# Side-by-side heads in the second block's attention, and buffers rounded up to 128 bytes, in a kernel of two transformer blocks

## What is computed

```python
for qb in range(s_len // Q_BLOCK):                  # Q_BLOCK = 128, two blocks
    start = qb * Q_BLOCK; end = start + Q_BLOCK
    z = jnp.einsum('bqhd,bkhd->bhqk', qi, kj) * scale   # keys 0 to end
    causal = s_pos < t_pos
    log_beta = jax.nn.log_sigmoid(z)
    log_rem = jnp.where(causal, jax.nn.log_sigmoid(-z), 0.0)
    suffix = lax.cumsum(log_rem, axis=3, reverse=True) - log_rem
    weights = jnp.where(causal, jnp.exp(log_beta + suffix), 0.0)
    o = jnp.einsum('bhqk,bkhd->bqhd', weights, vj)
```

## Time and profile before

| | |
|---|---|
| median of 3 runs | 1494.0 us (1493.9 to 1494.48) |
| the profiled execution | 1494.16 us, its span 1492.4 us |
| PE busy, of the span | 1156.6 us, 77% |
| PEld busy | 687.6 us, 46% |
| DVE busy | 503.9 us, 34% |
| ACT busy | 374.6 us, 25% |
| mean granted clock of PE | 0.878 of full speed |
| moved by DMA | 493.31 MB, 331 GB/s over the span |

### The profile page before, as it was taken

One profiled execution on the slowest core, in us unless ns is written; L12 is line 12 of the kernel. 1 busy time (PEld: TensorE's weight loads), 2 busy tenths in 40 slices (PEclk: granted clock), 3 DMA queues, 4 the chain that ended last, 5 costly groups with the idle time before them and its releaser, 6 DMA issues.

```text
span 1492.4 us, 19792 instructions
## 1 busy us (share of the span) xinstructions
PE 1156.6 (77%) x8185; PEld 687.6 (46%) x8185; DVE 503.9 (34%) x926; ACT 374.6 (25%) x618; POOL 41.0 (3%) x95
## 2 busy tenths in 40 slices
PE   8999999865666666556766566666666999999998
PEld 8787887321212212112112112122122778999887
DVE  6988895101101101001011011010110677676546
ACT  6658563100001001001001000000000564465434
POOL 1220120000000000000000000000000000000000
PEclk9999999988778778888688878778777999999999
DMA  8663429999999999999999999999999663455551
GB/s 303 198 253 113 184 85 365 392 427 427 426 426 429 427 428 426 429 429 427 427 427 427 428 428 428 428 428 426 428 428 425 209 214 114 170 188 179 198 177 49
DMA packets 58616, 493.31 MB, mean 331 GB/s; under 512 B 6666, under 2 KB 8260, under 8 KB 33988
## 3 DMA queue, kind: packets, MB, share of 16 engines
q1 hardware_dynamic: 57620, 491.54, 81.1%
q10 hardware_dynamic: 944, 1.05, 0.2%
HBM read 491.52 MB, written 1.05 MB: 330 GB/s over the span
## 4 chain that ended last, share of the span: by engine, by line
DMA 54%; PE 40%; DVE 4%; ACT 1%; issue 1%; SPq 0%; DVEq 0%; ACTq 0%
DMA arena<-in_expert_w_down 19%; DMA arena<-in_expert_w_up 18%; DMA arena<-in_expert_w_gate 17%; PE ps L1860 13%; PE ps L1951 7%; PE ps L1865 6%; PE ps L2307 4%; PE ps L2325 1%; DVE w_split L1145 1%; PE ps L1930 1%; PE ps L2121 1%; PE ps L2152 1%; PE ps L2384 1%; PE ps L2065 0%; PE ps L2040 0%
## 5 line engine op out<-in xcount | busy, mean ns | idle before, releaser
L2307 PE MATMUL ps<-ring,arena 128*32 128x512 f32 x1024 | 168.2, 797 | 89.6 <-DMA ring<-in_expert_w_up 61.0
L1145 DVE TENSOR_TENSOR w_split<-ring,w_split 128x1024 fp32r<-128x1024 f32 (+3 forms) x178 | 201.0, 1136 | 103.3 <-ACT w_split L721 102.1
L2307 PE MATMUL ps<-arena 128*32 128x512 f32 x1024 | 163.0, 779 | 90.2 <-DMA arena<-in_expert_w_up 59.9
L721 ACT ACTIVATE w_split<-ring 128x1024 fp32r<-128x1024 f32 (+3 forms) x178 | 175.4, 990 | 192.2 <-PE ps L1865 133.2
L1596 DVE TENSOR_TENSOR arena<-arena,ps 128x512 f32<-128x512 f32 x16 | 11.0, 688 | 504.1 <-PE ps L2307 504.1
L1603 DVE TENSOR_TENSOR xs<-ps,xs 128x512 f32<-128x512 f32 x64 | 39.8, 684 | 288.3 <-PE ps L2333 288.3
L2307 PEld LDWEIGHTS ps<-ring,arena 128*32 128x32 f32 x1024 | 33.9, 133 | 217.1 <-DMA ring<-in_expert_w_up 103.0
L2307 PEld LDWEIGHTS ps<-arena 128*32 128x32 f32 x1024 | 32.9, 128 | 211.3 <-DMA arena<-in_expert_w_up 98.5
L1951 PE MATMUL ps<-hT_hi,w_split 128*128 128x256 f32 x608 | 112.7, 286 | 0.2 <-DVE arena L1767 0.2
L2325 PE MATMUL ps<-arena 128*32 128x256 f32 x1056 | 77.1, 440 | 38.3 <-DMA arena<-in_expert_w_down 35.3
L2325 PE MATMUL ps<-ring,arena 128*32 128x256 f32 x928 | 74.1, 475 | 36.8 <-DMA ring<-in_expert_w_down 32.3
(11 more groups left out here) (361 smaller groups left out, 1383.7 us busy)
## 6 DMA issues: line engine op xcount, KB each, us to landing
arena<-in_expert_w_gate SPq DMA_DIRECT2D x35, 2048.0 KB, 35.8
ring<-in_expert_w_up SPq DMA_DIRECT2D x35, 2048.0 KB, 36.2
ring<-in_expert_w_gate SPq DMA_DIRECT2D x29, 2048.0 KB, 36.6
arena<-in_expert_w_up SPq DMA_DIRECT2D x29, 2048.0 KB, 37.2
arena<-in_expert_w_down SPq DMA_DIRECT2D x25, 2048.0 KB, 33.8
ring<-in_expert_w_down SPq DMA_DIRECT2D x21, 2048.0 KB, 34.6
ring<-in_w_ff SPq DMA_DIRECT2D x32, 1024.0 KB, 5.0
ring<-in_w_in SPq DMA_DIRECT2D x24, 1024.0 KB, 5.0
```

The lines of the kernel that those rows point to most:

```text
L721: act.activation(w_split[:, n % WBUFS, 0, 0:cols], slot_view(slot, cols)[:, n % 2, :], ACT.Copy).then_inc(split_hi, 1)
L1145: dve.tensor_tensor(buf[:, 1, :], w, buf[:, 0, :].bitcast(F32), ALU.subtract).then_inc(split_lo, 1)
L2307: m = pe.matmul(ps[j * CAP:(j + 1) * CAP, bank, :], xe[:, kt, :], w[:, r, j * FCOL:(j + 1) * FCOL], start=kt == 0, stop=kt == KT - 1, skip ...
```

## The change

`sb` rounds each buffer up to 128 bytes where it rounded to 32. In `pair_scores` the two loops change places: the scores of both heads are issued side by side, then the two masks, first for 128 and then for 256 columns. In `pair_output` the products of both heads over 256 columns come first, then both over 128. The number and the shapes of the instructions stay as they were, and so do the waits and what the last matmul signals.

```diff
-            used[0] += (math.prod(shape[1:]) * 4 + 31) // 32 * 32
+            used[0] += (math.prod(shape[1:]) * 4 + 127) // 128 * 128
...
                 pe.wait_ge(taken_ready, p)
-                for m in range(2):
-                    r = slice(SHD * m, SHD * (m + 1))
-                    for at_col, width, t0 in ((0, P, 0), (P, T, P)):
+                for at_col, width, t0 in ((0, P, 0), (P, T, P)):
+                    for m in range(2):
+                        r = slice(SHD * m, SHD * (m + 1))
                         pe.matmul(ps[:, 4 + m, at_col:at_col + width], qkT2[r, p, t0:t0 + P], qkT2[r, p, 2 * T - width:2 * T], start=True, stop=False)
+                    for m in range(2):
                         last = pe.matmul(ps[:, 4 + m, at_col:at_col + P], ident_r[:, :], never[:, :], start=False, stop=True)
                 last.then_inc(z_done, 1)
...
                 pe.wait_ge(wT_ready, p + 1)
                 pe.wait_ge(y_pair, p)
+                rows = [slice(SHD * m, SHD * (m + 1)) for m in range(2)]
+                heads = [slice((2 * p + m) * SHD, (2 * p + m + 1) * SHD) for m in range(2)]
                 for m in range(2):
-                    u = 2 * p + m
-                    r = slice(SHD * m, SHD * (m + 1))
-                    w = wT[p % 2][:, m, :]
-                    pe.matmul(ps[r, 3, 0:T], v2[:, 0, u * SHD:(u + 1) * SHD], w[:, 0:T], start=True, stop=False,
+                    pe.matmul(ps[rows[m], 3, 0:T], v2[:, 0, heads[m]], wT[p % 2][:, m, 0:T], start=True, stop=False,
                               skip_group_check=True)
-                    last = pe.matmul(ps[r, 3, P:T], v2[:, 1, u * SHD:(u + 1) * SHD], w[:, T:SC], start=False, stop=True,
+                for m in range(2):
+                    last = pe.matmul(ps[rows[m], 3, P:T], v2[:, 1, heads[m]], wT[p % 2][:, m, T:SC], start=False, stop=True,
                                      skip_group_check=True)
                 last.then_inc(yb_done, 1)
```

## The result

The kernel after takes 1484.15 us (median of 4, 1483.51 to 1485.34), the kernel before beside it on the same chip 1494.24; the ratio is 0.9928, its 95% interval 0.9916 to 0.994. The profiled execution took 1483.69, its span 1482.0.

The account below looks back on a forecast made before the run. DMA was taken to bound the expert stage and PE the second block's attention. Scores and clock, capped by DVE at 6.5 us, plus 0.6 for loads gave 7.1: 1486.9 from a median of 1494.0, range 1486.1 to 1489.6.

Parts of the forecast that it names:

- Part 1: Blocks of scores in the attention: both heads side by side, a block from 3.10 to 1.78 us, 5.3 us in four.
- Rival B: Scores in the attention: the two heads don't overlap, only turns are saved, a block 2.44 us, 1489.3 or 1491.4; chance 0.11.
- D: Whole edit: does nothing in time, as the engine looks ahead by itself, 1494; chance 0.03.
- Part 2: Output products in the attention: head 1 already runs beside head 0, so the new order wins 0 us.
- Part 3: Clock behind the fourth block of scores: denser blocks avoid its fall, winning 1.5 us.
- Rival A: Clock: it still falls once, PE gains 5.3 us and the buffers 0.6, 1488.1; chance 0.14.
- Part 4: Gating product in the attention: PE waits for DVE's L1695, 0.3 us comes back, PE gains at most 6.5.
- Part 5: Buffers moved onto multiples of 128 bytes: 96 arena loads in the expert stage quicker by 0.007 us each, 0.6 us.
- On the engines I count nothing: Engines' work on moved buffers: 0 us, as a chunk's 16 records take 1.92 us from ring and arena alike.
- The 0.6 us of the loads: Arena loads in the expert stage: 96 loads each 0.007 us quicker, bounds 0 and 1.0 us.
- Rival C: Expert stage: engines' reads meet DMA writes at the same offset, arena loads slow down, 1501.5 at 3%; chance 0.04.
- the rule on 256 bytes: Arena loads: descriptors not starting on 256 bytes fetch an additional piece; arena becomes as quick as ring, sum unchanged.

## Why the prediction was wrong

**Part 1, right.** Block 1.79 us (1.78 forecast), gain 1.31 for each of four; without a fall the attention takes 35.41 - 30.33 = 5.1 us less, which is 5.3 less the wait of 0.24 at the gating product. A mask behind a mask took 0.37 - 0.26 = 0.11, as chosen. Rival B, no overlap, and D, no effect, are out: four records of scores take the time of two.

**Part 2, right.** Nothing, in the change and alone.

**Part 3, half.** The amount is right, 1.5 us where the clock falls (36.91 - 35.41), but one profile was taken for the kernel's nature: the fall is there in three of five profiles with the old scores. It was worth some 0.9 us in the mean, not 1.5. The reason given (sparse blocks) isn't shown. Rival A took the fall for something of the changed kernel; it didn't come there.

**Part 4, right.** PE waited at L2442 for L1695, 1.97 - 1.73 = 0.24 us (0.3 forecast), and no other wait came up. With shorter blocks that wait grew to 0.95 and nothing was won. 

**Part 5, the step that failed: "On the engines I count nothing".** The term was put at 0 and measured 3.2 us in the tail. It rested on one row pair, 1.92 us for 16 records from the ring and from the arena. Those are the expert products, in which the buffer is the moving operand. The dense products of `down`, `out2` and the embedding have the arena as the stationary operand and w_split as the moving one, and those I had not compared. The evidence stood in before's trace: 395 ns with `fT`, 390 with `hT`, same line, same shape, same moving buffer, 504 matmuls on the path to the end, and in the chain 0.93 us for four with `fT`, 0.91 for four with `hT`. Read then, 504 x 0.0065 = 3.3 us would have made the forecast 1483.6 for the 1484.15 measured. In the first block `cT` gave another 0.3 us or so: L2065's first group starts at 110.63 instead of 110.92. The 0.6 us of the loads were right in size by the distances, 96 x 0.006; the lead fell by 0.7 with `cT`'s 0.3 in it, but it moves by more than that from one execution to the next and can't confirm it. Rival C is out (arena loads got no slower). The arena became as quick as the ring (4.8952 both). The prediction read this out of the rule on 256 bytes; but that rule has the same piece for 32 past as for 128 past, so the sign that it was said to give came from the rows alone. Where it does tell two places apart, at 256, lay another 6.35 us.

In sum: 7.1 forecast, 0.4 less in the attention (6.1 for 6.5, the clock), 0.1 more in the lead and 3.2 more in the tail give 10.0; measured 10.1. The 0.1 in the lead is no finding. That the one profile of before had a fall in it, as two of its three have, was luck for the forecast: from the profile without one the same reckoning would have had at most 5.3 for the attention, where 6.1 were measured in the mean. One slip stands in the range: with 6.5 at most from the attention and 1.0 from the loads its quick end is 1486.5, and no term gives the 0.4 below that.

## What to carry over

When a change moves buffers, go through all groups of instructions that touch them, once for each operand's role, and compare the mean of one between a moved and an unmoved buffer of the same shape: the trace of before often holds both. Place the operands of a hot matmul at the same place within 256 bytes (for 256 columns, measure: L1951 was a little quicker elsewhere) and buffers that big loads write on multiples of 256. And before a single fall of the clock enters a sum, profile the same kernel a second time.

## What the runs showed of the hardware

- 128x512 matmuls in fp32r follow each other in 0.227 us when stationary and moving operand start at the same place within 256 bytes (0, 128 or 160, all three tried), and in 0.232 to 0.235 when they differ by 32, 96, 128, 160, 192 or 224: 1.85 to 1.88 us instead of 1.81 for eight. Where in 128 or 256 bytes they both stand made no difference.
- Loads of 2 MB landed every 4.84 to 4.86 us in buffers that start on a multiple of 256 bytes, every 4.890 to 4.896 where the buffer starts 128, 160 or 192 past one, every 4.900 to 4.902 at 32 past.
- Float32 products of two heads in separate halves of the rows (scores) overlap: four records take the 0.42 and 0.63 us that two took. In separate halves of the columns (outputs) the records of both heads start in pairs. For the outputs it made no difference in which order the two heads were written (0.80 and 0.81 us), for the scores with their masks between it made 1.31 us a block.
- The granted clock fell to near half (0.52) for about 3 us in some executions of the same kernel and not in others, at a cost of 1.5 us.
